# A bank addition moved on VectorE, and a sixth seven-product block per half, in the w_down stage of a decoder layer

## What is computed

```python
    x = x + y @ w_out

    h = rms_norm(x, ffn_norm)
    return x + (jax.nn.silu(h @ w_gate) * (h @ w_up)) @ w_down
...
    return rms_norm(x, final_norm)
```

## Time and profile before

| | before |
|---|---|
| three timed runs, us | 1107.88, 1110.89, 1111.1 (median 1110.89) |
| profiled execution, its own time | 1110.28 us |
| its span, first to last instruction | 1108.6 us |
| mean granted TensorE clock | 0.997 of full speed |
| TensorE matmuls busy | 1094.4 us (99%) |
| VectorE busy | 833.1 us (75%) |
| ScalarE busy | 600.3 us (54%) |
| load of one w_down pair, issue to landing (median) | 4.8 us |
| w_down stage within the span | about 862 to 1101.7 us |

### The profile page before, as it was taken

One profiled execution on the slowest core, in us unless ns is written; L12 is line 12 of the kernel. 1 busy time (PEld: TensorE's weight loads), 2 busy tenths in 40 slices (PEclk: granted clock), 3 DMA queues, 4 the chain that ended last, 5 costly groups with the idle time before them and its releaser, 6 DMA issues.

```text
span 1108.6 us, 13405 instructions
## 1 busy us (share of the span) xinstructions
PE 1094.4 (99%) x5161; PEld 909.4 (82%) x5161; DVE 833.1 (75%) x760; ACT 600.3 (54%) x593; POOL 38.0 (3%) x44
## 2 busy tenths in 40 slices
PE   9999999999999999999999999999999999999997
PEld 6788889997888888888888888888888888788876
DVE  6444457664576798898898898898888878898793
ACT  6644346656655555454554555555554656475552
POOL 0380000000000000000000000000000000000000
PEclk9999999999999999999999999999999999999998
DMA  9765644653445555555555555556555655555551
GB/s 348 257 190 191 194 143 127 200 181 115 152 153 189 187 193 192 196 201 207 189 194 196 212 192 190 194 192 219 189 189 197 233 215 190 190 190 192 214 201 76
DMA packets 58323, 212.53 MB, mean 192 GB/s; under 512 B 4016, under 2 KB 11952, under 8 KB 41008
## 3 DMA queue, kind: packets, MB, share of 16 engines
q1 hardware_dynamic: 56288, 206.58, 54.0%
q10 hardware_dynamic: 2000, 5.46, 1.3%
HBM read 209.93 MB, written 2.10 MB: 191 GB/s over the span
## 4 chain that ended last, share of the span: by engine, by line
PE 93%; DVE 2%; DMA 2%; ACT 1%; issue 1%; SPq 0%; DVEq 0%; ACTq 0%
PE ps L1498 59%; PE ps L1274 9%; PE ps L1276 9%; PE ps L1275 9%; PE ps L1313 2%; DMA raw<-in_w_in 1%; DMA raw<-in_w_dn 1%; PE ps L1411 1%; PE ps L1361 1%; PE ps L1462 1%; PE ps L1464 1%; PE ps L1463 1%; PE ps L1360 0%; DVE mix L1227 0%; ACT w_hi L409 0%
## 5 line engine op out<-in xcount | busy, mean ns | idle before, releaser
L1498 PE MATMUL ps<-w_hi,xp_hi 128*128 128x512 f32 x539 | 211.7, 393 | 0.0
L1498 PE MATMUL ps<-w_hi,xp_lo 128*128 128x512 f32 x539 | 209.9, 389 | 0.0
L1498 PE MATMUL ps<-w_lo,xp_hi 128*128 128x512 f32 x539 | 209.7, 389 | 0.0
L816 DVE TENSOR_TENSOR w_lo<-raw,w_hi 128x2048 fp32r<-128x2048 f32 (+2 forms) x44 | 91.9, 2088 | 87.9 <-ACT w_hi L409 87.9
L1008 DVE TENSOR_TENSOR w_lo<-raw,w_hi 128x2048 fp32r<-128x2048 f32 x55 | 125.8, 2287 | 34.5 <-ACT w_hi L621 34.5
L621 ACT ACTIVATE w_hi<-raw 128x2048 fp32r<-128x2048 f32 x55 | 105.1, 1911 | 62.2 <-DMA raw<-in_w_gu 62.2
L1274 PE MATMUL ps<-w_hi,xT_hi 128*128 128x512 f32 (+1 forms) x352 | 132.7, 377 | 1.2 <-DVE w_lo L816 1.2
L1276 PE MATMUL ps<-w_hi,xT_lo 128*128 128x512 f32 (+1 forms) x352 | 131.0, 372 | 0.0
L1275 PE MATMUL ps<-w_lo,xT_hi 128*128 128x512 f32 (+1 forms) x352 | 130.9, 372 | 0.0
L710 ACT ACTIVATE w_hi<-raw 128x2048 fp32r<-128x2048 f32 (+1 forms) x44 | 80.1, 1821 | 85.2 <-DMA raw<-in_w_dn 85.1
L1498 PE MATMUL ps<-w_hi,xo_hi 128*128 128x512 f32 x302 | 118.5, 392 | 3.6 <-DVE ps L1132 3.6
(11 more groups left out here) (235 smaller groups left out, 1867.1 us busy)
## 6 DMA issues: line engine op xcount, KB each, us to landing
raw<-in_w_gu SPq DMA_DIRECT2D x88, 1024.0 KB, 4.8
raw<-in_w_dn SPq DMA_DIRECT2D x44, 1024.0 KB, 4.8
raw<-in_w_in SPq DMA_DIRECT2D x34, 1024.0 KB, 5.1
raw<-in_w_out SPq DMA_DIRECT2D x16, 1024.0 KB, 5.1
raw<-in_w_in SPq DMA_DIRECT2D x8, 576.0 KB, 3.8
raw<-in_w_ukv SPq DMA_DIRECT2D x3, 1024.0 KB, 5.1
raw<-in_w_uq SPq DMA_DIRECT2D x3, 768.0 KB, 4.4
xT_raw<-in_xT SPq DMA_DIRECT2D x4, 512.0 KB, 8.3
```

The costliest lines, as they stand in the source:

```text
L816: nc.vector.tensor_tensor(w_lo[n % 4][:, 0:k, 0:c], raw[n % 4][:, 0:k, 0:c], w_hi[n % 4][:, 0:k, 0:c].bitcast(F32), ALU.subtract).then_inc ...
L1498: mm = nc.tensor.matmul(out, x, wt, start=start and j + m == 0, stop=stop and 3 * j + m == n - 1, skip_group_check=resumed)
```

## The change

In each half of w_down six pairs instead of five are blocks, at q = 0, 4, 7, 10, 13, 16 instead of 0, 4, 8, 12, 16. And VectorE's second in-place addition stands in step q = 16, right after the second residual sum and ahead of `down_lo(m + 3)`, instead of at the head of step q = 17. The pair whose end it waits for is the same one, pair 17 of the half (`DN0 + m + 2` seen from one step earlier).

```diff
-DSUMS = (0, 4, 8, 12, 16)
+DSUMS = (0, 4, 7, 10, 13, 16)
...
                     mix_banks(FS + h, 0, None)
                     residual(h, 1)
-                if q == DSUMS[-1] + 1:
-                    mix_banks(FS + h, 1, DN0 + m + 1)
+                    mix_banks(FS + h, 1, DN0 + m + 2)
                 if m == DQ - 1:
```

## The result

| | before | changed |
|---|---|---|
| median, us | 1111.06 (five runs, 1107.88 to 1111.31) | 1103.14 (five runs, 1102.02 to 1103.76) |
| ratio to before | 1 | 0.9932 (95% interval 0.9917 to 0.9947) |
| profiled execution, its own time | 1110.28 | 1103.76 |
| span | 1108.6 | 1102.0 |
| matmuls in the trace | 5161 | 5155 |

The forecast was 1103.3 us. The page's first part of the changed kernel answers to the earlier trace rows: six matmuls fewer, and 11.0 us more of VectorE.

A forecast was written before the change was run, and what follows sets the result against it. TensorE was taken to bound the kernel, waiting in w_down only for the second bank additions. 5.87 us (gaps and low clock) plus 1.36 (six matmuls) gave 7.2 off 1110.28, 1103.0 profiled, so a median of 1103.3; range 1101.3 to 1106.8.

The forecast's parts named there:

- Where the bound is: In w_down TensorE sets the end almost everywhere; a matmul taken out is worth 0.2267 us.
- the two gaps: TensorE's waits in w_down for the late second bank addition, one per half: 2.16 us and 1.97 us.
- the sum: Whole gain forecast in w_down: 5.87 us from the moved addition plus 1.36 from the blocks, 7.2 us.
- The price of the gap: At pair 18 of both halves, by matmul spacing: 2.16 + 1.97 + 1.74 = 5.87 us, against 3.6 us of waits.
- The clock's share: Slow matmuls at the 1.2 GHz level behind half 1's gap: 1.74 us, said to go with the gap.
- the first rival: Clock's share in w_down not in the timed runs: gain of 5.5 us, to 1105.4; chance 0.15.
- low stretch: Twelve matmuls behind half 1's gap taking 4.46 us where 2.72 were due, at the 1.2 GHz clock level.
- The move costs nothing: Second bank addition ahead of pair 19's low parts: wait for pair 17 holds nothing, nothing else becomes late.
- the spares of 0.9 and 0.8 us: Time left before TensorE wants the moved addition's banks (0.9 us) and pair 19's low part (0.8 us).
- The sixth block: One more block per half of w_down: six matmuls fewer, 1.36 us; extra VectorE and ScalarE work costed at nothing.
- The range: Time range from 1101.3 us to 1106.8, the high end taking in the first rival and most of the second.
- whether VectorE becomes the bound: Slower rival: late preparation at blocks 7, 10, 13, 16 stops TensorE eight times; 1114.2 us and above; chance 0.04.

The follow-up runs named there:

- e1_move: Against the kernel before: only the second bank addition moved, five blocks per half kept; 1104.66 us against 1109.1, ratio 0.9954.
- e4_seven_late: Against the changed kernel: seven blocks per half, crowded at the end (0, 4, 7, 10, 12, 14, 16); 1107.42 us, ratio to before 0.9982.
- e2_blocks: Against the kernel before: six blocks per half, second bank addition left where it was; 1108.35 us against 1109.1, ratio 0.9992.
- e6_pad_two: Against the changed kernel: one added VectorE scratch instruction of 128 x 1024 ahead of the second bank addition; 1104.86 us.
- e7_pad_long: Against the changed kernel: five added VectorE scratch instructions of 128 x 1024 ahead of the second bank addition; 1118.42 us, ratio to before 1.0078.

## Why the prediction was right

**Where the bound is.** Right. Of all of TensorE's time in w_down only the two gaps were open, and e1_move shows their price: 5.92 us of w_down for 5.87 in the sum. What is left is all accounted for: 12 blocks of 4.76 us and 32 pairs of 5.44 make 231.0 us from first to last start, and the other 1.1 of the changed kernel's 232.05 lie almost all in the first two pairs, where TensorE has some matmuls of `ident` by `gate` in between, in every version alike.

**The price of the gap.** Right, and this was the step that mattered. The view of waits gives 3.6 us for the two waits; the distance of the matmuls round them gives 5.87. Of the difference of 2.3 us some 0.7 is what the view of waits doesn't book (2.16 us lost for 1.84 booked in half 0, of that 0.1 a slow first distance, 0.34 us for 0.227, behind the gap), the rest the clock.

**The clock's share.** Right for the profiled execution, and only partly for the timed runs; the first rival holds part of the truth. Before ran 44 times in the three sessions. In 22 runs the mean granted clock was 0.998 or 0.999, with a median of 1109.06 us; in 15 it was 0.997 (median 1110.65); in 6 it was 0.995 (median 1112.08); one run stands apart (0.946, 1110.85). The steps are of one size, about 1.5 us, which is what one low stretch costs in the trace (1.55, below), so 0.997 is read here as one fall and 0.995 as two; only the trace at 0.997 shows its one fall. By this reading the clock fell in 21 of 43 runs. The kernels without the gap (the changed kernel in both sessions, e1_move and the kernel of the spread blocks in both) had 0.998 or 0.999 in all of their 27 executions. Against undisturbed runs of before the change gains 1109.06 - 1103.26 = 5.8 us, where the rival had 5.5; against all 44, whose median is 1109.4, 6.2; against the first five, whose median has a fall in it, 7.9. The time itself, 1103.1 for 1103.3, owes little to this: the sum starts from an execution with one fall and takes that fall off. That the gain in the medians came out at 7.9 for the 7.6 of the forecast is in part luck: another five runs of before would as often as not have had a median some 1.5 us lower, and then the gain is that of the first rival. What the sum had mis-sized is small: it priced the low stretch at 1.74 us, but half 1's gap would have cost 2.16 like half 0's without it, so the stretch is 1.97 + 1.74 - 2.16 = 1.55.

**The move costs nothing.** Right: the wait for pair 17 held nothing, and the spares of 0.9 and 0.8 us were measured by using them up: 0.95 and 0.8.

**The sixth block.** Right: 1.28 and 1.37 us between e1_move and two traces of the changed kernel for 1.36, nothing lost on VectorE, the idle times within 0.05 us, the spare of the blocks 1.5 to 1.85 us for 1.8. VectorE had 11.0 us more to do for 11.7, ScalarE 2.8 for about 4. The estimate by the rule of the Trainium skill ("VectorE: DVE Perf Modes", section on the TRN2 errata), 9.04 us for a block's ten instructions, was for the durations one after the other. The booked durations of block 12's ten instructions do add up to 9.00 us. But the trace has 8.66 from the first one's start to the start of the next pair's work, since most of them start before the booked end of the one before. So the row was the better value, and the narrow 0.1 us that the rule left ahead of the second plain pair was 0.61.

**The range.** The low end is said to be the lowest time less 5.5 with some rounding, but 1107.88 - 5.5 is 1102.4; the further 1.1 us down to 1101.3 is not worked out. It didn't matter: the median is 1103.14, and no run of the changed kernel went below 1102.02. The step that was least sure, whether VectorE becomes the bound, had a margin of over 1 us at these places and none at others, which e4_seven_late shows.

## What to carry to other kernels

Price a stall of the bounding engine by the distance between its instructions before and behind it, not by the wait that is booked: a gap of 2.0 us cost 2.2, and 3.7 where the clock fell. When an engine that works in order is late with one short step, look at what stands ahead of it in its program; moving 1.1 us of work ahead of 2.8 us that was not yet due gave 4.4 us in the medians against undisturbed runs of before (e1_move), and 5.9 against the execution in which the clock fell. And count blocks that load a helper engine by their distances, not by their number: seven in 22 cost TensorE no wait when spread and cost 5.6 us when crowded.

## What the runs showed of the hardware

- The granted clock falls behind some gaps of TensorE and not behind others of the same length, in the same program. By the mean granted clock (0.997 and below), it fell with two gaps of 2.0 us in 21 of 43 runs of before, leaving out the one that stands apart, and in six of twelve of e2_blocks; with two of 2.9 to 3.1 us in eight of ten; with two of 5.5 us (5.4 booked) in all four, behind both in the trace. With gaps of 1.1 us and less (e4_seven_late, e6_pad_two) it was 0.998 or 0.999 in all eleven. What decides for one gap or another the runs don't show.
- A fall does not cost the same behind every gap: about 1.55 us behind a gap of 2.0 us (eight slow distances between matmuls, 0.427 us instead of 0.227), about 2.7 us behind one of 3.1 (14 of them). Nor does it come at the same point: in the trace of before the clock was still 1.00 when the matmuls had come back (1080.6 to 1081.5), and the first slow distance begins at 1081.79, 1.1 us after the gap's end; in e7_pad_long it fell within the gap. Each of these is read from one trace.
- A change that removes such a gap also removes spread: 1102.02 to 1103.76 us in ten runs of the changed kernel, 1107.67 to 1112.48 in 44 of before (1107.67 to 1109.80 in the 22 in which the clock didn't fall).
